# Norm factors by logarithm and exponential instead of root and reciprocal, in a three-block FP32 kernel

## The reference

```
for i in range(2):
    x = x + 0.5 * swiglu(rmsnorm(x), ...)          # width 2816
    h = rmsnorm(x) @ w_in[i]
    y = [rmsnorm(mla(h)), rmsnorm(silu(layernorm(conv31(h)))), rmsnorm(hyena(h))]
    x = x + y @ w_out[i]
    x = x + 0.5 * swiglu(rmsnorm(x), ...)
x = second block: x + (gate_a * ssm(h) + gate_b * attention(h)) @ w_mix_out, then swiglu
out = rmsnorm(x)

def rmsnorm(x, g):
    return x * lax.rsqrt(jnp.mean(x * x, axis=-1) + 1e-6) * g
```

## Time and profile before

| | |
|---|---|
| Three runs | 3360.20, 3362.32, 3365.25 us, median 3362.32 |
| The profiled execution | span 3360.4 us from its first to its last instruction; no other time of it is given |
| PE busy | 3228.2 us, 96% of the span |
| POOL, DVE, ACT busy | 1835.2 us (55%), 1812.3 us (54%), 748.6 us (22%) |
| Granted clock of TensorE, mean | 0.987 of full speed |
| All waits of PE on DVE | largest: for `x_lo` L1717 21.6 us in 10 places |
| All waits of PE on ACT | largest: for `square` L1432 13.7 us in 28 places |

### The profile page before, as it was taken

How to read it: one execution, slowest core, us unless ns; L and a number is a source line. 1 busy time by engine, 2 the same in 40 slices (tenths; PEclk the granted TensorE clock), 3 DMA queues, 4 the chain that set the end, 5 groups by cost and what they waited for, 6 DMA issues and landing times.

```text
span 3360.4 us, 44069 instructions
## 1 busy us (share of the span) xinstructions
PE 3228.2 (96%) x14534; PEld 2578.4 (77%) x14534; DVE 1812.3 (54%) x1971; ACT 748.6 (22%) x1260; POOL 1835.2 (55%) x1026
## 2 busy tenths in 40 slices
PE   8999998899999999999889999999999999999998
PEld 6788875578888778876567888788777877888886
DVE  7661277663313765138754331586768886753312
ACT  2110126422201111014532220111122322222200
POOL 5556651066666656663036666644455455666665
PEclk9999999999999999999999999999999999999999
DMA  4222320022323322331012222322122222223322
GB/s 155 81 86 96 113 76 26 9 86 94 100 94 103 110 79 89 100 107 56 13 44 88 98 96 98 118 76 69 63 85 69 76 69 70 94 94 94 97 96 81
DMA packets 77430, 281.26 MB, mean 84 GB/s; under 512 B 9382, under 2 KB 9766, under 8 KB 76776
## 3 DMA queue, kind: packets, MB, share of 16 engines
q1 hardware_dynamic: 74016, 268.58, 24.5%
q10 hardware_dynamic: 3272, 10.79, 0.9%
HBM read 277.24 MB, written 2.10 MB: 83 GB/s over the span
## 4 chain that ended last, share of the span: by engine, by line
PE 79%; DVE 15%; issue 4%; ACT 2%; DVEq 0%; DMA 0%; ACTq 0%; SPq 0%
PE bank L505 24%; PE bank L510 23%; PE bank L509 23%; DVE short L1938 1%; PE bank L640 1%; PE bank L725 1%; PE bank L790 1%; DVE square_sum L1727 1%; DVE xbc L2276 1%; DVE y L1970 1%; DVE x_lo L1717 1%; DVE scaled L2114 1%; PE bank L799 1%; DVE att_qk L2212 0%; DVE reach L2369 0%
## 5 line engine op out<-in xcount | busy, mean ns | idle before, releaser
L451 POOL TENSOR_SCALAR w_hi<-raw 128x1024 fp32r<-128x1024 f32 x504 | 554.8, 1101 | 1451.4 <-PE bank L505 1443.0
L454 POOL TENSOR_TENSOR w_lo<-raw,w_hi 128x1024 fp32r<-128x1024 f32 x504 | 1267.5, 2515 | 42.0
L505 PE MATMUL bank<-x_hi,w_hi 128*128 128x512 f32 x2896 | 1151.3, 398 | 47.7 <-DVE x_lo L1717 21.6
L510 PE MATMUL bank<-x_hi,w_lo 128*128 128x512 f32 x2896 | 1134.6, 392 | 0.0
L509 PE MATMUL bank<-x_lo,w_hi 128*128 128x512 f32 x2896 | 1134.0, 392 | 0.0
L505 PEld LDWEIGHTS bank<-x_hi,w_hi 128*128 128x128 f32 x2896 | 547.8, 189 | 183.4 <-issue 66.4
L510 PEld LDWEIGHTS bank<-x_hi,w_lo 128*128 128x128 f32 x2896 | 547.6, 189 | 116.2
L509 PEld LDWEIGHTS bank<-x_lo,w_hi 128*128 128x128 f32 x2896 | 547.8, 189 | 114.5 <-issue 4.1
L505 PE MATMUL bank<-hidden_hi,w_hi 128*128 (+1 forms) x880 | 342.3, 389 | 0.0
L509 PE MATMUL bank<-hidden_lo,w_hi 128*128 (+1 forms) x880 | 342.3, 389 | 0.0
L510 PE MATMUL bank<-hidden_hi,w_lo 128*128 (+1 forms) x880 | 342.3, 389 | 0.0
(11 more groups left out here) (382 smaller groups left out, 3229.1 us busy)
## 6 DMA issues: line engine op xcount, KB each, us to landing
raw<-in_w SPq DMA_DIRECT2D x504, 512.0 KB, 3.6
dft<-in_dft ACTq DMA_DIRECT2D x2, 1536.0 KB, 6.6
out<-x SPq DMA_DIRECT2D x4, 512.0 KB, 2.6
mask<-in_mask ACTq DMA_DIRECT2D x1, 1536.0 KB, 7.2
x<-in_x SPq DMA_DIRECT2D x2, 512.0 KB, 5.9
x<-in_x SPq DMA_DIRECT2D x1, 1024.0 KB, 8.8
filt_cos<-in_dft_filter ACTq DMA_DIRECT2D x2, 512.0 KB, 6.5
filt_sin<-in_dft_filter ACTq DMA_DIRECT2D x2, 512.0 KB, 8.1
```

Of the source, the lines that this page charges most:

```text
L451: nc.gpsimd.tensor_scalar(w_hi[:, s % 2, :], raw[:, s, :], 1.0, 0.0, ALU.mult, ALU.add).then_inc(w_rounded, 1)
L454: nc.gpsimd.tensor_tensor(w_lo[:, s % 2, :], raw[:, s, :], w_hi[:, s % 2, :].bitcast(F32), ALU.subtract).then_inc(w_split, 1)
L505: first = nc.tensor.matmul(out, hi_w, hi, start=start, stop=False)
L510: return nc.tensor.matmul(out, lo_w, hi, start=False, stop=stop)
```

## The change

Root and reciprocal become a logarithm and an exponential, both on ACT: exp(-0.5 ln(scale * sum + eps)). DVE's reciprocals of norm factors go, and DVE's waits for ACT's semaphore stay or move to the result. `norm_rms` counts 4 per layer instead of 6, and the two latent factors count on `latent_inverted` directly. PE's 12 idle matmuls behind the last head go; its wait for `probs_ready`, which stood in the same call, stays.

```
+            def inverse_root(to, squares, scale):
+
+                link(nc.scalar.activation(to, squares, ACT.Ln, bias=eps[:], scale=scale))
+                return nc.scalar.activation(to, to, ACT.Exp, scale=-0.5)
...
             def rms():
                 act.wait_ge(sum_ready, c.next(sum_ready))
-                nc.scalar.activation(rstd[:], bank[SUM_BANK][:], ACT.Sqrt, bias=eps[:], scale=1.0 / D
-                                     ).then_inc(rms_ready, 1)
+                inverse_root(rstd[:], bank[SUM_BANK][:], 1.0 / D).then_inc(rms_ready, 1)
...
-                    nc.scalar.activation(latent_root[:], bank[SUM_BANK][:, 0:TT], ACT.Sqrt, bias=eps[:],
-                                         scale=1.0 / width).then_inc(norm_rms, 1)
+                    inverse_root(latent_root[:], bank[SUM_BANK][:, 0:TT], 1.0 / width).then_inc(latent_inverted, 1)
...
                 def root(at, width, to):
                     act.wait_ge(norm_sum, c.next(norm_sum))
-                    nc.scalar.activation(to[:], bank[at][:], ACT.Sqrt, bias=eps[:], scale=1.0 / width
-                                         ).then_inc(norm_rms, 1)
+                    inverse_root(to[:], bank[at][:], 1.0 / width).then_inc(norm_rms, 1)
...
-            def reciprocal_rms():
+            def factor_taken():
                 dve.wait_ge(rms_ready, c.next(rms_ready))
-                link(nc.vector.reciprocal(rstd[:], rstd[:]))
...
-                latent_inverse()
+                dve.wait_ge(latent_inverted, c.next(latent_inverted))
                 gate_tiles()
                 latent_scale((2,), KV_NORM)
                 gate_product(0)
                 norm_squares(2, lambda: long_taps(2))
-                long_taps(2)
-                latent_inverse()
-                long_taps(3)
+                long_taps(5)
+                c.add(latent_inverted)
...
-                def inverted(rms):
+                def factor_ready():
                     dve.wait_ge(norm_rms, c.next(norm_rms))
-                    link(nc.vector.reciprocal(rms[:], rms[:]))
...
-                inverted(mix_rms)
+                factor_ready()
                 scale_tiles([y[:, 2 + i, :] for i in range(CT)], OUT_NORM + 2, mix_rms)
-                inverted(late_rms)
                 remainders((0, 1))
+                factor_ready()
...
-                run_idle(6, SCORE_BANKS[0], probs_ready, 32)
+                after(probs_ready, 32)
                 after(norm_split, 3 + 2)
-                after(norm_rms, 4)
+                after(norm_rms, 2)
                 out_pair(0, 0)
...
-                after(norm_rms, 6)
+                after(norm_rms, 4)
                 out_pair(1, 0)
```

More of the change, by code:

```diff
@@ L1516, in mixer @@
                 act.wait_ge(ln_sum, c.next(ln_sum, 2))
-                nc.scalar.activation(late_rms[:], bank[HYENA_BANKS[0]][:], ACT.Sqrt, bias=eps[:], scale=1.0 / CW
-                                     ).then_inc(norm_rms, 1)
+                inverse_root(late_rms[:], bank[HYENA_BANKS[0]][:], 1.0 / CW).then_inc(norm_rms, 1)
                 turned(7, 2)
@@ L1939, in short_tile @@
                                                             short[:, i, :], ALU.mult, ALU.add))
-                def latent_inverse():
-                    dve.wait_ge(norm_rms, c.next(norm_rms))
-                    nc.vector.reciprocal(latent_root[:], latent_root[:]).then_inc(latent_inverted, c.add(latent_inverted))
                 def latent_scale(tiles, at):
@@ L2243, in attention_slot @@
                     value_tile(2, VALUE_TILE_BANK)
-                if j == 0:
-                    link(nc.vector.reciprocal(first_rms[:], first_rms[:]))
                 normalise(2 * j)
@@ L2407, in ssm_group @@
                 arrive(4 if g else 5)
-                dve.wait_ge(root_ready, c.next(root_ready))
-                nc.vector.reciprocal(root_cols[:], root_cols[:]).then_inc(root_inverted, c.add(root_inverted))
                 def scale(i):
@@ L2540, in _ @@
             ffn(7, 1.0, last=True)
-            dve.wait_ge(rms_ready, c.next(rms_ready))
-            nc.vector.reciprocal(final_root[:], final_root[:]).then_inc(root_inverted, c.add(root_inverted))
             dve.wait_ge(root_spread, c.next(root_spread))
```

59 lines of the change are left out of this document (20 added, 39 removed).

## The result

| | before | changed |
|---|---|---|
| Median of the runs | 3362.36 us (13 runs) | 3369.1 us (13 runs) |
| Lowest and highest | 3359.42, 3365.75 | 3365.91, 3376.76 |
| Ratio, with its 95% interval | | 1.0021 [1.0013, 1.0029] |
| The profiled execution | span 3360.4 | 3366.6 us, span 3364.8 |
| Granted clock of TensorE, mean | 0.987 | 0.985 |

The changed kernel is 6.7 us slower, 0.2%, which is the least that the prediction takes for a difference; the interval lies clear of 1. 3375.9 was predicted, range 3364 to 3384: direction and range held, the size was about half of what was forecast.

What follows compares the result with a forecast made beforehand. PE was taken to bound the kernel (79% of the chain, DVE 15%). Terms 4.8 - 2.7 + 8.8 + 2.2 + 0.6 - 1.4 + 1.3 = +13.6, added to the median 3362.3, gave 3375.9 us, range 3364 to 3384.

Steps and rivals of the forecast that it cites:

- One load serves both functions: Rival, at every factor: one table load covers logarithm and exponential, 1.28 us less each time; 3347.5 us, chance 0.05.
- A switch costs more than its load: Rival, at added loads on the path: ACT also drains about as long as it loads; 3398 us, chance 0.01.
- First latent factor: Tile 5 of the input projection: the factor comes later and PE stands idle, +2.4 us per layer, +4.8 in all.
- A fall of the clock in the input projection: Behind the new 2.4 us gap in tile 5: even odds of a 2.2 us clock drop in each layer, +2.2.
- End of the mixer without the clock: Mixer's end and output projection: -0.35 at the first piece, +3.9 before piece (1, 0), -4.9 remainder waits; -1.35 per layer, -2.7.
- The clock there: Output projections: without idle matmuls the clock drops behind two gaps per layer, 2.2 us a drop, +8.8.
- the clock holds: Rival: no clock drops in output or input projections, sum +2.6, 3364.9 us, no measurable change; chance 0.24.
- Attention: Factor that opens the attention: comes 1.4 us sooner and PE's wait for it goes, -1.4, bounds -1.4 and 0.
- final norm: Last norm of the kernel: its factor comes later and nothing covers it, +1.3 us.
- state-space: State-space groups: only the first group's factor comes late for PE, the other three are hidden; +0.6, bounds 0 and 2.4.
- The seven wide factors: Wide factors ahead of networks and mixers: no effect, as PE projects unscaled inputs meanwhile and no wait leads to them.

Runs made afterwards that it cites:

- both logarithms first: Changed kernel with both logarithms ahead of both exponentials in each pair of factors at the mixer's end, PE released by the logarithms: 3358.54 us, 0.999.
- the experiment on the latents alone: Kernel before with only its two latent factors by logarithm and exponential, all idle matmuls kept: 3361.86 us, 0.9997.
- both logarithms first, others by root, 4 idle: Kernel with both logarithms first and other factors by root, plus 4 idle matmuls behind the last head, ahead of piece (0, 0): 3349.06 us, 0.9961.
- changed, idle in three places: Changed kernel with idle matmuls ahead of head 7's last mixed product, behind that head and ahead of piece (1, 0): 3367.11 us, 1.0006.
- both logarithms first, others by root: Kernel with both logarithms first, with latents, mixer's first norm, state-space groups and final norm back at root and reciprocal: 3355.16 us, 0.9981.
- before, 4 idle: Kernel before with 4 idle matmuls behind the last head instead of 12, nothing else: 3367.48 us, 1.0018.
- before, none: Kernel before with only its 12 idle matmuls behind the last head removed, roots and reciprocals kept: 3366.79 us, 1.0011.

## Why the prediction was half right

- **One load serves both functions**: fell. 25 and 25 loads at 1283 ns; the Trainium skill's page "ScalarE: Activation LUTs", under "Table sets: the hidden batching unit", has one load for a logarithm and an exponential behind it, and this program has two at each factor. The trace disagrees; in this program the two functions behave as if of two sets. Seen so, the rule of the same section to batch by set agrees with the runs: with both logarithms first the pair has two loads for four, and some 10 us went, PE's earlier release included, which alone brought nothing that can be seen.
- **A switch costs more than its load**: fell. Load to activation is 0.02 (433.58 + 1.28 = 434.86, next at 434.88), logarithm to load 0.11 with the wait for itself (434.88 + 0.26 = 435.14, then 435.25). The 1.38 us of drain that the same page of the Trainium skill gives under "What ACT_TABLE_LOAD costs" is not to be seen.
- **First latent factor**, +2.4 a layer: the mechanism and nearly the size were right, +2.2, and PE's wait 1.92 (the spread follows ACT's end by 0.14, where 0.38 was put in). The sentence that followed it was wrong: "From there DVE works without a pause to the mixer's heads, so the delay reaches them whole." It reaches them (+2.0 and +1.9 in the experiment on the latents alone), and the heads give it back (-3.3 and -2.0), with shorter stretches of the lower clock. The latents alone changed the time by nothing that can be measured: 0.9997 where +4.8 us would be 1.0014. This is the first step that failed; it put the heads at 0, a stretch of fixed length. Why the stretches come out shorter is not shown.
- **A fall of the clock in the input projection**, even odds: in six kernels with late latents it came 6 times in 12 layers behind the first spread (1 of 2 in the changed one), so the odds were right. But the term counted only what the change adds. In the kernel before and the five kernels without late latents the clock falls in 5 of 12 input projections as well, there behind the second latent's column sums (L890), as at 450 in the profile of before (0.57 over 450 to 454), and no layer of any profile has both. The difference of the odds, and so the term, is near nothing: -0.5 was measured for +2.2.
- **End of the mixer without the clock**, -1.35 a layer: right step by step where the clock held (-0.3 to +0.1 for -0.35, +3.9 for +3.9, -4.4 and -4.5 for -4.9). The total of -1.34 in layer 1 is luck, as said above.
- **The clock there**, four falls: all four came, so "the clock holds" fell. 2.2 each was put in. Behind the head 2.4 to 2.7 were measured, so that price was right. Behind piece (1, 0) it was 0.9 to 1.0: the term was mis-sized at "PE bounds this stretch, so it is lost whole", which fails there. PE is busy for only 3.51 of 6 us at 665 to 671, where the rows have 5.87 of 7, and 0.8 of what the low clock loses is a wait that stood ahead of the last four pieces anyway. The four make 7.0 for 8.8.
- **Attention** -1.4, measured -1.7; **final norm** +1.3, measured +1.3; **state-space** +0.6, with waits of 0.4 twice at L1193. The seven wide factors at nothing: no wait of PE leads to them.

By terms, in the profiles: +4.4 for the latents, -0.5 for the rest of the input projection, -5.3 in the heads, +2.7 for the end of the mixer, -1.7, +1.3, and a rest of +3.3, of which the wait behind each output projection and the fall at 2391 are the most. Against the forecast of 13.6 the end of the mixer is 3.3 less (2.1 less in the column sums, 1.8 less by the clock's price, 0.6 more in the rest), the input projection's clock 2.7 less and the heads 5.3 less, and the rest is 2.7 more, which no term had. The number is half right because these partly cancel. How much of the heads' share is due to the change, and how much to the one profile of before that all offsets are taken from, stays open: some kernels without late latents had it too, in part. Nor do single parts add up: without idle matmuls +4, latents alone 0, everything but the latents (and the norm ahead of the mixer) 0, all together +6.7. With some 1 to 3 us per layer that hang on how PE's waits fall in time, differences of that size between two kernels are not to be explained instruction by instruction.

## What to carry to other kernels

Ahead of replacing a reciprocal by a second activation, count table loads on the way from the sum to whoever waits: here a wide factor that stood alone came 1.3 to 1.7 us sooner, a narrow one 1.3 to 2.2 later, and two wide ones behind each other held PE for 5 us until their logarithms were put side by side. Idle matmuls are priced by the gap that is left behind them, so they have to be re-fitted after every change near them: 12 were worth 4 us in one place, 4 were worth nothing there and some 3 in another. And a delay on the bottleneck engine need not arrive at the end, where the granted clock between is not the same for both. Before a fall of the clock is put on a change's bill, look for falls at the same place in the kernel before: the input projection had as many with root and reciprocal, only a little later.

## What was not expected of the hardware

The gap in front of a dense stretch and what the clock did then, at piece (0, 0) of the first layer (time of the first matmul: 0.47 at the upper level, 0.77 at the lower):

| kernel | PE's waits inside head 7 | PE idle before the piece | first matmul | clock behind |
|---|---|---|---|---|
| before | 1.1 | 0.76 | 0.47 | held |
| both logarithms first, others by root, 4 idle | 1.9 | 0.48 | 0.47 | held |
| changed, idle in three places | 2.4 | 0.39 | 0.47 | held |
| both logarithms first | 1.9 | 2.21 | 0.47 | fell within the piece |
| both logarithms first, others by root | 1.9 | 2.21 | 0.47 | fell within the piece |
| changed | 4.1 | 2.21 | 0.77 | had fallen |
| changed, PE released by the logarithm | 4.7 | 2.21 | 0.77 | had fallen |
| changed, latents and first norm by root | 4.4 | 2.31 | 0.77 | had fallen |
| before, 4 idle | 1.1 | 4.02 | 0.77 | had fallen |
| before, none | 1.3 | 5.70 | 0.77 | had fallen |

At 2.21 us the clock was still up at the first matmul in the two kernels whose head 7 has few waits and down in the others, and in all it fell; so a wait of this length costs a fall here though 3.12 us at 687.48 between dense stretches did not the earlier trace rows. And the unforeseen part: the same wait of 3.58 us in the same head is followed by a window at 0.53 in one kernel and at 0.81 in another, where it comes 2.6 us earlier, though the instructions around it are the same. Likewise the 3.29 us ahead of piece (1, 0), in one and the same execution, were followed by a piece at full clock in layer 1 and by the lower level in layer 2. What decides between the two was not found.
